# Opening loads in order of need, gate weights held stationary, and a last head that takes over work of its out projection

## What is computed

```python
mod = (c_act @ ada_w[layer] + ada_b[layer])[:, None, :]
sh_a, sc_a, gt_a, sh_m, sc_m, gt_m = jnp.split(mod, 6, axis=-1)
h = modulate(rms_norm(x, attn_norm[layer]), sh_a, sc_a)     # rms_norm(x) * (1 + scale) + shift
# differential attention, 8 heads of width 128, two score maps each
q, k, v = jnp.split(h @ w_in, 3, axis=-1)
a = p[:, :, 0] - lam_full * p[:, :, 1]                      # p: softmax of scores + bias
o = rms_norm(einsum(a, v), subln) * (1 - lam_init)          # per head
x = x + gt_a * (o.reshape(B, T, 1024) @ w_out)
# before the second attention: shared keys and values, compressed ones, and the gates
gates = jax.nn.sigmoid((h @ w_in)[..., H * d:])             # 48 columns: 16 heads x 3 branches
```

## Time and profile before

| quantity | value |
|---|---|
| median of 3 runs | 2359.68 us (2350.24, 2359.68, 2361.68) |
| the profiled execution's own time | 2350.47 us |
| its span, first to last instruction | 2348.6 us |
| TensorE busy | 2230.7 us, 95% |
| DVE busy | 1225.4 us, 52% |
| ACT busy | 509.4 us, 22% |
| mean granted clock | 0.978 |
| moved by DMA | 452.79 MB, mean 193 GB/s |

### The profile page before, as it was taken

The page is one execution under the profiler, slowest core; times in us unless marked ns, Lnnn a source line. Parts: engine busy times, 40 slices in busy tenths (PEclk is TensorE's granted clock), DMA queues, the critical chain, the costliest instruction groups (busy, mean ns, idle before and its releaser), DMA issues. The chain is left out here.

```text
span 2348.6 us, 26613 instructions
## 1 busy us (share of the span) xinstructions
PE 2230.7 (95%) x9826; PEld 1501.9 (64%) x9826; DVE 1225.4 (52%) x2808; ACT 509.4 (22%) x1164; POOL 40.9 (2%) x48
## 2 busy tenths in 40 slices
PE   6999899999999999999999999999999899999976
PEld 4444588888888645557888888854669444444332
DVE  5355377667777255667655667668556311111104
ACT  3223213231002144442333100022332100000001
POOL 0000000000000000000000000000000000010100
PEclk8999899999999999999999999999999899999998
DMA  8555223344443111122444453421022799999996
GB/s 324 214 197 197 72 72 142 145 188 171 160 198 117 54 36 55 54 81 108 179 186 172 158 201 144 183 104 72 1 103 113 276 427 426 427 427 424 427 427 248
DMA packets 45171, 452.79 MB, mean 193 GB/s; under 512 B 7496, under 2 KB 7496, under 8 KB 19952
## 3 DMA queue, kind: packets, MB, share of 16 engines
q1 hardware_dynamic: 37616, 435.71, 46.5%
q0 software_dynamic: 6240, 12.17, 1.4%
q10 hardware_dynamic: 1184, 3.19, 0.3%
HBM read 444.08 MB, written 17.87 MB: 197 GB/s over the span
## 5 line engine op out<-in xcount | busy, mean ns | idle before, releaser
L1267 PE MATMUL ps<-big,ring 128*128 128x256 f32 x768 | 186.0, 380 | 0.6 <-PE ps L1182 0.6
L1182 PE MATMUL ps<-hT,ring 128*128 128x256 f32 x768 | 178.6, 381 | 0.0
L3135 PE MATMUL ps<-big 128*64 128x512 f32 (+1 forms) x416 | 169.9, 598 | 7.8 <-ACT big L3190 5.0
L1182 PEld LDWEIGHTS ps<-hT,ring 128*128 128x128 f32 x768 | 144.9, 190 | 23.3 <-ACT hT L437 4.3
L1267 PEld LDWEIGHTS ps<-big,ring 128*128 128x128 f32 x768 | 145.8, 190 | 20.7 <-issue 1.4
L555 PE MATMUL ps<-hT,ring 128*128 128x512 f32 x336 | 151.6, 601 | 0.0
L3135 PE MATMUL ps<-ring,big 128*64 128x512 f32 (+1 forms) x336 | 134.1, 595 | 11.4 <-ACT big L3190 6.6
L2186 PE MATMUL ps<-hT,ring 128*128 128x512 f32 x320 | 140.7, 594 | 2.7 <-DVE big L2568 1.7
L1079 DVE SCALAR_TENSOR_TENSOR ring<-ring,tmp 128x1024 f32<-128x1024 f32 x112 | 136.4, 1219 | 0.0
L1267 PE MATMUL ps<-oT 128*128 128x256 f32 x512 | 120.9, 380 | 2.1 <-DVE oT L1446 2.1
L1182 PE MATMUL ps<-oT 128*128 128x256 f32 x512 | 115.8, 380 | 0.0
(11 more groups left out here) (540 smaller groups left out, 3897.1 us busy)
## 6 DMA issues: line engine op xcount, KB each, us to landing
ring<-in_stream SPq DMA_DIRECT2D x99, 2048.0 KB, 8.7
big<-in_up SPq DMA_DIRECT2D x18, 2048.0 KB, 22.8
ring<-in_down SPq DMA_DIRECT2D x17, 2048.0 KB, 22.4
ring<-in_gate SPq DMA_DIRECT2D x15, 2048.0 KB, 23.4
big<-in_gate SPq DMA_DIRECT2D x10, 2048.0 KB, 20.7
big<-in_down SPq DMA_DIRECT2D x8, 2048.0 KB, 22.3
ring<-in_up SPq DMA_DIRECT2D x6, 2048.0 KB, 19.6
oT<-in_up SPq DMA_DIRECT2D x5, 2048.0 KB, 28.5
```

Of the source, the lines that this page charges most:

```text
L1182: ins = pe.matmul(place(i, name), a[:, k, :], b[:, k, :], start=(k == 0), stop=(k == 3))
L1267: ins = pe.matmul(m.ps[:, bank[name], q * H:(q + 1) * H], a[:, q * P:(q + 1) * P], b, start=(first and q == 0), stop=(final and q == 1))
L3135: ins = pe.matmul(out[a:z, :], left[:, k * P + a:k * P + z], bufs[j][:, k * width + c * 512:k * width + (c + 1) * 512], start=(k == 0), st ...
```

## The change

1. **Opening.** vec and con are reordered so that what the opening needs is at their front. `phase_start` loads only these columns, then x, chunk 0, half of head 0's weights (the 384 columns used), chunk 1, the other half, chunk 3. The bias product goes ahead of the condition product. Only modulation chunk 0 is worked there; ACT loads the root's table ahead, and keep-busy products stand before and after the sums. In `phase_diff` SP loads chunk 4, bias tables, chunk 5 and the rest of vec and con; DVE multiplies tiles by the inverse root alone (`unit_rows`) and forms the columns of chunks 1 to 3 in between; ACT forms gain and shift per tile and applies both at once.
2. **Last heads.** Variances of heads 0 to 3 are taken in head 5 (`rooting`), with ACT switching to the root and back. Their norms are applied during head 6 (`norming`). In head 7 TensorE takes the four P1 products of `out_a`, ACT copies them, and DVE forms weight sums 0 (end of head 6) and 1 (end of head 7). `phase_residual` for `out_a` starts with tiles 4 to 7 and P2.
3. **Gates.** The gate weights are stationary, 48 columns, in two halves of the array's columns; even feature tiles go to partitions 0 to 47 of the bank, odd ones to 64 to 111. ACT copies the result with tokens reversed in each block, four small products add the halves and turn them, and ACT applies the sigmoid from PSUM. The flip product and DVE's copy are gone.

The diff, cut to its core (`sum_weights` gathers the four operations that stood in two places):

```diff
-    for name, n in (("c", 8), ("c2", 8), ("ada_b0", 48), ("ada_b1", 64), ("ada_b2", 48),
-                    ("attn_norm0", 8), ("attn_norm1", 8), ("mlp_norm0", 8), ("mlp_norm1", 8),
+    for name, n in (("c", 8), ("c2", 8), ("ada_b0", 48), ("attn_norm0", 8), ("subln", 1), ("lam", 256), ("rel_bias", 16),
+                    ("ada_b1", 64), ("ada_b2", 48), ("attn_norm1", 8), ("mlp_norm0", 8), ("mlp_norm1", 8),
...
-    for name, n in (("ident", 128), ("tri_ones", 512), ("neg_upper_t", 128), ("neg_future", 128),
-                    ("bucket", 512), ("cmp_neg", 128), ("cmp_ok", 128), ("tri_strict", 128),
+    for name, n in (("ident", 128), ("bucket", 512), ("tri_ones", 512), ("neg_upper_t", 128), ("neg_future", 128),
+                    ("cmp_neg", 128), ("cmp_ok", 128), ("tri_strict", 128),
...
+def first_head_half(m, sp, half, done):
+    n = STREAM["diff"][0] + DIFF_ORDER.index(("head", 0))
+    ks = slice(4 * half, 4 * half + 4)
+    part = lambda a: a.rearrange("p (k n) -> p k n", k=KT)[:, ks, 0:384]
+    sp.dma_start(part(m.ring[:, n % RING, :]), part(m.stream[n])).then_inc(done, 16)
...
-                sp.dma_start(m.vec[:], m.d_vec).then_inc(small, 16)
-                sp.dma_start(m.con[:], m.d_con).then_inc(consts, 16)
+                sp.dma_start(m.vec[:, 0:VEC_FIRST], m.d_vec[:, 0:VEC_FIRST]).then_inc(small, 16)
+                sp.dma_start(con(m, "ident"), m.d_con[:, 0:P]).then_inc(consts, 16)
+                sp.dma_start(buckets(m.con), buckets(m.d_con)).then_inc(consts, 16)
                 sp.dma_start(m.xT[:], m.d_x.rearrange("(k p) t -> p k t", p=P)).then_inc(xin, 16)
-                load_stream(m, sp, 0, RING)
-                prefetch(m, sp, "ada_a")
+                load_stream(m, sp, 0, 1)
+                first_head_half(m, sp, 0, m.head_in)
+                load_stream(m, sp, 1, 2)
+                first_head_half(m, sp, 1, m.full[2])
+                load_stream(m, sp, 3, 4)
...
-                act.wait_ge(bias_sb, 3)
-                act.dma_start(m.d_rel, rb).then_inc(m.rel_out, 16)
+                act.activation(m.rs[:, 0:1], m.eps2[:], ACT.Sqrt)
...
-                act.wait_ge(m.rel_out, 16)
-                for h in range(2):
-                    for mm in range(2):
-                        act.dma_start(diff_rel(m)[:, h, mm, :], m.rel_tab(2 * h + mm)).then_inc(m.rel_in[h], 16)
...
-                for c in range(n):
-                    chunk, full, v = ring_chunk(m, at + c)
-                    dve.wait_ge(full, v)
-                    for j in range(4):
-                        o = first_column(c, j)
-                        modulation_tile(m, dve, at + c, j, crow, m.mod0[:, o:o + 1]).then_inc(mod_done, 1)
-                    dve.wait_ge(mod_done, 4 * (c + 1))
-                    dve.sem_inc(m.free[(at + c) % RING], 1)
-                    if c == 0:
-                        dve.wait_ge(rooted, 1)
-                        dve.reciprocal(m.st[:, 0:NT], m.st[:, 0:NT]).then_inc(inverse, 1)
-                first_gains(m, dve, c1, 0, 2 * n)
+                dve.wait_ge(m.full[0], 16)
+                for j in range(2):
+                    first_modulation(m, dve, 0, j, crow).then_inc(mod_done, 1)
+                dve.wait_ge(rooted, 1)
+                dve.reciprocal(m.st[:, 0:NT], m.st[:, 0:NT]).then_inc(inverse, 1)
+                for j in range(2, 4):
+                    first_modulation(m, dve, 0, j, crow).then_inc(mod_done, 1)
+                dve.wait_ge(mod_done, 4)
+                dve.sem_inc(m.free[0], 1)
...
-                pe.wait_ge(consts, 16)
+                pe.wait_ge(consts, 32)
+                pe.matmul(m.ps[0:16, 0, :], fl(m, "rel_bias", BUCKETS), con(m, "bucket", BUCKETS),
+                          start=True, stop=True).then_inc(bias_mm, 1)
...
                 pe.wait_ge(m.go, 3)
+                pe.wait_ge(bias_sb, 3)
+                keep_busy(m, pe, 0, 4)
                 for k in range(0, KT, 2):
...
                 last.then_inc(summed, 1)
+                keep_busy(m, pe, 0, 6)
                 pe.wait_ge(inverse, 1)
                 spread_rows(m, pe, m.ps[:, 7, :], m.st[:, 0:NT])
...
                 n0 = at + RING
+                load_stream(m, sp, 4, 5)
+                sp.wait_ge(m.rel_out, 16)
+                load_rel(0)
+                load_stream(m, sp, 5, 6)
+                load_rel(1)
+                sp.dma_start(m.vec[:, VEC_FIRST:N_VEC], m.d_vec[:, VEC_FIRST:N_VEC]).then_inc(m.rest_in, 16)
+                sp.dma_start(m.con[:, CON_FIRST:N_CON], m.d_con[:, CON_FIRST:N_CON]).then_inc(m.rest_in, 16)
                 load_stream(m, sp, n0, n0 + 3)
...
-                    pe.wait_ge(m.full[n % RING], 16 * (n // RING + 1))
+                    pe.wait_ge(m.head_in, 16)
                     for k in range(KT):
+                        if k == 4:
+                            pe.wait_ge(m.full[n % RING], 16 * (n // RING + 1))
                         pe.wait_ge(h_ok, k + 1)
...
+                    if h == 0:
+                        pe.wait_ge(m.rest_in, 32)
...
+                def head_norm(n):
+                    pe.wait_ge(inverse, 1)
+                    if n == 0:
+                        pe.wait_ge(tr_a, 2 * norming - 1)
+                    elif n == 1:
+                        pe.wait_ge(tr_d, norming)
+                    else:
+                        pe.wait_ge(normed, n - 1)
+                    spread_rows(m, pe, m.ps[:, 5 + n % 2, :], m.st[:, NT * n:NT * (n + 1)]).then_inc(spread, 1)
+                def first_product(p):
+                    if p == 0:
+                        pe.wait_ge(k_sb, heads)
+                        pe.wait_ge(normed, early)
+                    elif p == 2:
+                        pe.wait_ge(v_tok, heads)
+                    if p % 2 == 0:
+                        _, full, value = ring_chunk(m, out_at + p // 2)
+                        pe.wait_ge(full, value)
+                    w = out_quarters(m, out_at, p)[0]
+                    for k in range(4):
+                        last = pe.matmul(m.ps[:, out_bank(p), 256 * (p % 2):256 * (p % 2) + 256], w[:, k, :], oT[:, k, 0:256],
+                                         start=(k == 0), stop=(k == 3))
+                    last.then_inc(first_out, 1)
...
                     scores(h, 3)
                     if more:
                         project(h + 1, 0, 0, half)
+                    else:
+                        first_product(0)
+                    if h == norming:
+                        head_norm(0)
                     scores(h, 2)
                     if more:
                         project(h + 1, 0, half, KT)
+                    if h == norming:
+                        head_norm(1)
                     scores(h, 1)
                     if h:
                         head_squares(h - 1)
                     if more:
                         project(h + 1, 2, 0, half)
+                    if h == norming:
+                        head_norm(2)
                     scores(h, 0)
                     if more:
                         project(h + 1, 2, half, KT)
+                        if h == norming:
+                            head_norm(3)
                         project(h + 1, 1, 0, KT)
+                    else:
+                        for p in range(1, 4):
+                            first_product(p)
+                    if h == norming:
+                        pe.wait_ge(normed, early)
                     finish(h)
...
-                shift_rows(act, outs, hs, h_ok)
+                for k in range(KT):
+                    if k >= 2:
+                        act.wait_ge(first_done, 2 * k - 2)
+                    act.activation(m.gain[:, k:k + 1], m.mod0[:, 8 + k:9 + k], ACT.Identity, scale=fl(m, "attn_norm0")[:, k:k + 1],
+                                   bias=m.gain[:, 8 + k:9 + k]).then_inc(gain_ok, 1)
+                    act.activation(m.mod0[:, k:k + 1], m.mod0[:, k:k + 1], ACT.Identity, bias=fl(m, "ada_b0")[:, k:k + 1]
+                                   ).then_inc(shift_ok, 1)
+                    act.wait_ge(unit, k + 1)
+                    act.wait_ge(gain_ok, k + 1)
+                    act.wait_ge(shift_ok, k + 1)
+                    act.activation(m.hT[:, k, :], m.hT[:, k, :], ACT.Identity, scale=m.gain[:, k:k + 1], bias=m.mod0[:, k:k + 1]
+                                   ).then_inc(h_ok, 1)
...
+                    if h == rooting:
+                        act.wait_ge(var_in, 1)
+                        act.activation(m.st[:, 0:NT * early], m.st[:, 0:NT * early], ACT.Sqrt).then_inc(rooted, 1)
+                        act.activation(m.rs[:, 0:1], m.eps2[:], ACT.Exp)
+                    if not more:
+                        first_copy(0)
...
+                    else:
+                        first_copy(1)
...
-                scale_rows(m, dve, outs, hs, range(4))
-                first_rows(2)
-                first_rows(3)
...
```

(64 more changed lines are left out.)

147 lines of the change are left out of this document (77 added, 70 removed).

## The result

The changed kernel takes 2325.72 us in the median (2323.24 to 2334.90), the kernel before 2360.68 (2350.24 to 2361.79): a ratio of 0.9869, 95% interval 0.983 to 0.9908. In a later comparison it was 2326.28 against 2361.28, 0.9857 (0.9838 to 0.9876). The profiled execution has 2325.73 us of its own, span 2324.0, mean granted clock 0.982. It stands at its median, while the profile of before stands 10 us under its own. So the medians are 35 us apart, the two profiles 24.7.

What follows compares the result with a forecast made beforehand. TensorE, 95% busy, bounds: gains need its idle time, low clock or removed work. Opening -6.6, heads and out projection -12, compression -6.4 sum to -25; against the old median 2334.7, rounded to 2334, range 2317 to 2347.

Steps and rivals of the forecast that it cites:

- Opening: Start to the end of head 0's projection: ends at 47.5 instead of 54.1, -6.6 us.
- S: Start of phase two in the opening, forecast at 23.5; the first projection was to end at S + 24.0.
- full clock in the opening: Rival: keep-busy products hold the clock through the sums, S = 21.0, opening -9.1, 2331 in all; chance 0.13.
- Head 6: Four spreads move into head 6, where TensorE never idles, 0.9 us each: +3.7 us.
- Last head: Last head's scores to the out projection's first spread: -1.8 up to the transposes, -1.7 behind, together -3.5 us.
- the fill: Last head: first product 0 fills TensorE's gap at 258 and delays the next scores by 0.6 us.
- products 1 to 3: Last head: these first products, 5.2 us, lie before the transposes and end at 268.5; DVE's combination is ready at 268.2.
- The rival with the low clock throughout: Rival: first products hold the last head, low clock throughout, finish 5 us later: 2340; chance 0.13.
- Out projection: First spread to P6: 13.3 us remain (spreads 6.3 at low clock, P2 6.9) of 23.65, -10.3 us.
- Stall: Out projection: two weight sums fewer on DVE, so the 2.27 us stall before 312.25 goes: -2.3 us.
- Compression: Compression phase: wide gate products in two column halves, 3.5 us, and next products at full clock: -6.4 us in sum.
- What I had at zero: Closing sums to the MLP, first MLP, second attention to `out_m`, and `out_m` and all behind: forecast difference 0.

Runs made afterwards that it cites:

- two tries on the kernel before: Kernel before, out projection's weight sums of group 3 moved on DVE behind u4 of group 0 (ratio 0.9994), then behind all of group 0 (2356.94 us).
- second edit: Kernel before with the weight sums of product group 3 moved behind the whole of group 0 on DVE in the first out projection: 2356.94 us, one run.

## Why the prediction was right

Forecast 2334, range 2317 to 2347, measured 2325.72. Between like executions I had put -25, and it is -24.7. Point by point:

**Opening: right in sum, two terms off.** -6.6 against -6.91, and -6.67 alone. (a) The squares did not start 4.0 us earlier but 2.7. x landed at 10.9 (issued at 2.14, 8.8 us to landing, 12.3 before), 3.1 earlier, and ACT was then busy with the condition rows until 11.4, which I had called in time. Their product started at 6.58, not near 5.3, behind the bias product that the change puts ahead of it (1.86 us). The Trainium skill, "DMA: Bandwidth & Descriptors", section Bandwidth, advises transfers of 1 MiB and more and calls those under 64 KB descriptor-dominated; from it I had estimated x about 1 us later than in my sum. The traces agree in size: in the three profiles where ACT waits for x itself (squares at 10.86, 11.38 and 11.89) it came 0.9 to 1.9 us later than my 10.0, though no run tells small transfers from other causes. (b) The spread took 1.29 us instead of 2.1, as the clock came back 0.5 us into it, which with a shorter second row made up for sums that ended at 18.89 instead of 17.9. From S on it was 24.05 us, forecast 24.0, but the agreement is partly luck. The 24.0 was DVE's chain, whose terms add up to 0.3 less than the 19.7 written for it, and DVE's rows took 0.63 us each, not 0.7. What bound was TensorE, the nearly tied limit: it multiplies without a pause from 24.87 to the end.

**Rival "full clock in the opening".** It is no separate case but one end of a scale: over nine profiles with this first row the sums took 4.92 to 6.99 us, and 4.38 with the longer first row. I had a chance on each of two outcomes, where the trace has a spread: the projection ended between 46.30 and 48.80 with the same opening code.

**Head 6: right.** +3.56, four spreads of 0.9.

**Last head: the fill is right, two terms are not.** -1.05 instead of -3.5 in the profile; -2.74 in the other profile of the same kernel (19.62 us), while four further kernels with this head have 21.3 again. The transposes were to start 11.6 us after the scores and started 14.18 after them. The first failed step is "products 1 to 3 (5.2 us)": they took 7 us in the one and 5.3 in the other, and I had put 1.7 for this case in the bounds only. The second is the time at which they and DVE are ready: the three products began 7.2 us after the scores in both profiles, where 268.5 less 5.2 means 6.4, and the combination that I had at 268.2, 11.3 us after the scores, came 12.3 after them. In before's trace 268.26 is where its last operation starts; it ends at 270.19. So even at full clock the transposes could not start before 12.3. Behind them the forecast held: 7.13 us to the spread against 9.01. The rival with the low clock throughout did not come.

**Out projection: right, a little under.** -11.6 against -10.3: the spreads, which I priced at low clock, were low for about 3 us of their length and took 5.28 instead of 6.3.

**Stall: the term that was mis-sized.** -4.1 against -2.3. I counted the idle time, 2.27, and not the product behind it, 3.57 us where the same form takes 1.89. Both were in the rows that I had before me. The two tries on the kernel before show that the second follows the first: 3.55 us for removing it.

**Compression: right.** -6.2 from the gate products on, forecast -6.4; the other 0.4 in the table is ahead of them, in unchanged work. The halves in series give +3.4, forecast 3.5.

**What I had at zero.** Closing sums +0.93, first MLP -1.82, `out_m` and after +1.9: unchanged code, where the clock fell or rose at another instant.

**The median.** My 2334 was the old median less 25; it came out 9 lower. The opening alone brings about 7.5 us in medians, and undoing the heads or the gates costs about 17 and 9, some 33 in sum. The stretches that changed give 26 in the two profiles. The rest lies in unchanged code: second attention to `out_m` takes 935.0 to 935.3 us in seven of 13 profiles and 936.9 to 943.4 in the others. Before's runs were mostly near 2360, a few near 2350; the two edited versions of before have 943.3 in that stretch, its own profile 935.02. So the profile that I summed against had the short stretch, and most runs of that kernel probably the long one. Of the eight profiles with the new gates, six have the short one (one of the changed kernel's own two); of the five with the old gates, one. In the three longest, all with old gates, 1.6 to 1.7 us is the slow start of the second attention told above. The rest of it is open: whether the change does this, or where its phases happen to fall, no run tells. I had seen the 9 us between profile and median and carried them over unchanged, which was the step that failed for the median.

## What to carry to other kernels

Price a stall together with the record behind it: look whether that record takes its usual time. When the clock is in play, take a product's price at both levels and ask what it delays at each; a product moved to where TensorE would else wait makes the length independent of the clock, at the price of a few tenths when the clock stays up. Compare a record's length with the same form elsewhere before calling its clock full. Read a ready time from the end of the last operation, not from its start. Sum against the profiled execution, but ask what separates it from the median before that difference is carried over.

## What the runs showed of the hardware

**The same code meets the clock at different instants.** Same kernel, same rows: the four spreads take 5.28 or 3.81 us, three products 7.13 or 5.45, the sums of the opening 5.58 or 5.08. The 20 us windows in an unchanged part show it between the kernel before and its second edit:

```profile
1740.00:1760.00 20.00, 19.03 (x119) 17.76 (x116) 11.49 (x17) 7.87 (x11) 0.00 (x0) 0.91 0.68 270
1120.00:1140.00 20.00, 19.50 (x111) 16.03 (x112) 13.76 (x20) 7.41 (x12) 2.57 (x3) 1.00 0.82 304
```

```profile
1740.00:1760.00 20.00, 19.03 (x111) 17.83 (x110) 8.73 (x16) 8.14 (x13) 0.00 (x0) 0.74 0.43 167
1120.00:1140.00 20.00, 19.50 (x98) 15.83 (x97) 13.54 (x20) 6.78 (x11) 2.57 (x3) 0.91 0.76 294
```

0.91 and 1.00 in the first, 0.74 and 0.91 in the second, where TensorE is as busy and does fewer records. From 780 to 1760 six of 49 such windows differ, in each the second kernel has the lower clock, and the shares missing add up to 12 us; its unchanged stretch, which ends inside the last window, is 8.3 us longer. The Trainium skill, "TensorE: Matmul & The Clock Gate", section The HAM clock gate, says that the window over which activity is watched is free-running, so that the same kernel shows different counts of slow products from run to run; the traces agree: the changed kernel's two profiles have 7.13 and 5.45 us for the same 24 records.

**The clock fell under a busy engine.** In six of the ten openings with the new code it fell 1.7 to 3.7 us after the one-column records had begun, in windows in which TensorE was busy throughout (14 to 17 above). In the other four it was low from the first of them or fell within 0.3 us. I had placed the fall near 13.5, 1.5 us into the sums as I had them; in the changed kernel it came 1.8 us into them.

**Column halves.** Two products of 48 stationary columns in different halves of the array take the time of one: 3.64 against 7.07 us for 16 records of 512 columns.
